# Scale and bias of the gating values: two GpSimd instructions become eight on VectorE

## What is computed

```python
def spatial_gating(z, ln_g, ln_b, w_s, b_s):
    u = z[..., :GMLP_WIDTH]
    v = layer_norm(z[..., GMLP_WIDTH:], ln_g, ln_b)      # 256 channels
    vs = v.reshape(bsz, n_s, GMLP_BLOCK, GMLP_HEADS, GMLP_HEAD_DIM)
    w = jnp.where(mask[None], w_s, 0.0)
    sv = jnp.einsum('hij,bsjhc->bsihc', w, vs) + b_s.T[None, None, :, :, None]
    return u * sv.reshape(bsz, t, GMLP_WIDTH)

def mixing_sublayer(x, ...):
    h = x @ w_in + b_in
    ...                                                  # c: conv group, att: attention
    gm = spatial_gating(jax.nn.gelu(h[..., OFF_GMLP:]), gmlp_ln_g, gmlp_ln_b, gmlp_w_s, gmlp_b_s)
    return jnp.concatenate([c, att, gm], axis=-1) @ w_out + b_out
```

## Time and profile before

| what | value |
|---|---|
| median of three runs | 943.93 us (942.88 to 945.69) |
| the profiled execution's own time | 938.3 us |
| its span in the profile | 936.5 us |
| mean granted clock of TensorE | 0.973 |
| TensorE busy with matmuls | 867.4 us (93%) |
| VectorE busy | 403.8 us (43%) |
| GpSimd busy | 300.3 us (32%) |

### The profile page before, as it was taken

One profiled execution on the slowest core, in us unless ns is written; L12 is line 12 of the kernel. 1 busy time (PEld: TensorE's weight loads), 2 busy tenths in 40 slices (PEclk: granted clock), 3 DMA queues, 4 the chain that ended last, 5 costly groups with the idle time before them and its releaser, 6 DMA issues.

```text
span 936.5 us, 15865 instructions
## 1 busy us (share of the span) xinstructions
PE 867.4 (93%) x5987; PEld 570.8 (61%) x5987; DVE 403.8 (43%) x924; ACT 253.6 (27%) x473; POOL 300.3 (32%) x223
## 2 busy tenths in 40 slices
PE   6999799889999998999999997998899999979995
PEld 5877578755555554555488776787555555545551
DVE  5997746732111111111559977467321111111126
ACT  5324842301111111111233248423012111111111
POOL 0632446222222221221534324462222222212233
PEclk9999899979999999999999998999799999999998
DMA  9761067799999999996814210677999999999955
GB/s 322 279 226 56 11 266 308 283 416 405 404 407 401 408 406 406 403 396 196 178 38 135 91 55 9 265 311 293 416 399 346 400 406 405 408 408 399 401 146 163
DMA packets 66278, 273.33 MB, mean 292 GB/s; under 512 B 8722, under 2 KB 24242, under 8 KB 41136
## 3 DMA queue, kind: packets, MB, share of 16 engines
q1 hardware_dynamic: 53792, 247.14, 66.1%
q0 software_dynamic: 12432, 25.41, 11.2%
HBM read 256.83 MB, written 22.02 MB: 298 GB/s over the span
## 4 chain that ended last, share of the span: by engine, by line
PE 65%; DVE 20%; DMA 10%; issue 2%; ACT 2%; POOL 0%; DVEq 0%; SPq 0%; ACTq 0%; POOLq 0%
PE bank L790 28%; PE bank L445 15%; PE bank L796 14%; DMA w_down<-in_exp_w_down 8%; DVE bank L1168 8%; PE bank L773 2%; DVE xTl L1137 2%; DMA moemem<-x_rows,first_tok 2%; DVE w_gate L1144 1%; PE bank L780 1%; PE bank L840 1%; PE bank L783 1%; DVE w_gate L1145 1%; DVE w_down L1143 1%; DVE xtok L1299 1%
## 5 line engine op out<-in xcount | busy, mean ns | idle before, releaser
L1414 DVE TENSOR_TENSOR moemem<-bank,moemem 64x128 f32<-64x128 f32 x172 | 48.3, 281 | 309.1 <-ACT moemem L1046 306.4
L1634 POOL DMA_INDIRECT moemem<-x_rows,gather_idx x43 | 44.9, 1045 | 284.5 <-DVE moemem L1428 260.4
L790 PE MATMUL bank<-w_up,moemem 128*64 128x256 f32 x1088 | 126.5, 386 | 2.2 <-DMA w_up<-in_exp_w_wide 2.2
L1581 POOL TENSOR_TENSOR wl<-w_gate,wh 128x2048 fp32r<-128x2048 f32 x17 | 78.0, 4590 | 126.4 <-ACT wh L909 98.4
L445 PE MATMUL bank<-xTh,wh 128*128 128x512 f32 (+1 forms) x256 | 101.1, 395 | 11.2 <-DVE xTl L1137 9.9
L790 PEld LDWEIGHTS bank<-w_up,moemem 128*64 128x64 f32 x1088 | 79.6, 140 | 47.1 <-issue 10.6
L1046 ACT ACTIVATE moemem<-bank 64x256 f32<-64x256 f32 x86 | 32.7, 381 | 246.3 <-PE bank L790 246.3
L445 PE MATMUL bank<-xTl,wh 128*128 128x512 f32 (+1 forms) x256 | 95.4, 373 | 0.0
L445 PE MATMUL bank<-xTh,wl 128*128 128x512 f32 (+1 forms) x256 | 95.2, 372 | 0.0
L1628 POOL DMA_INDIRECT y_rows<-moemem,scatter_idx x44 | 71.0, 1614 | 62.3 <-ACT moemem L1051 54.5
L790 PE MATMUL bank<-w_gate,moemem 128*64 128x256 f32 x736 | 83.4, 379 | 3.7 <-DMA w_gate<-in_exp_w_wide 3.7
(11 more groups left out here) (227 smaller groups left out, 1278.9 us busy)
## 6 DMA issues: line engine op xcount, KB each, us to landing
w_up<-in_exp_w_wide SPq DMA_DIRECT2D x24, 2048.0 KB
w_gate<-in_exp_w_wide SPq DMA_DIRECT2D x16, 2048.0 KB, 20.6
w_down<-in_exp_w_down SPq DMA_DIRECT2D x16, 2048.0 KB, 25.1
w_down<-in_exp_w_wide SPq DMA_DIRECT2D x8, 2048.0 KB
w_gate<-in_exp_w_down SPq DMA_DIRECT2D x8, 2048.0 KB
xtok<-in_exp_w_wide SPq DMA_DIRECT2D x8, 2048.0 KB, 24.4
moex<-in_exp_w_wide SPq DMA_DIRECT2D x8, 2048.0 KB
moew<-in_exp_w_down SPq DMA_DIRECT2D x8, 2048.0 KB
```

The lines of the kernel that those rows point to most:

```text
L790: return [pe.matmul(bank[i][CH * n:CH * n + CH, 0:256], x, w[:, 512 * n + 256 * i:512 * n + 256 * i + 256], start=(k == 0), stop=(k == KD ...
L1414: dve.tensor_tensor(he[CH * b:CH * b + CH, P * i:P * i + P], bank[i][0:CH, P * b:P * b + P], silu[:, 256 * i + P * b:256 * i + P * b + P], ...
L1581: pool.tensor_tensor(wl[(n + l) % SLOTS][:, :], wraw[n % 2], wh[(n + l) % SLOTS][:, :].bitcast(F32), ALU.subtract)\
L1634: return pool.indirect_dma_start(to, None, x1_halves[l], bass.IndirectOffsetOnAxis(ap=rows[:, :], axis=0), bounds_check=2 * T - 1, oob_is_ ...
```

## The change

GpSimd's two instructions go. VectorE's first four instructions no longer multiply by rstd but by `ln_g` (the first half of `rowm`), so they wait for `row_in` in place of `grstd_set`. Four further instructions multiply by rstd and add `ln_b`, in place in `gv`, behind `softmax_norm(l, 1)` and ahead of `heads_low(l, 0)`; each waits for the one before it (`link`). `gvn_set` is counted up behind them.

```diff
@@ VectorE
-                dve.wait_ge(grstd_set, l + 1)
-                for j in range(TT):
-                    link(dve.tensor_scalar(gv[:, j, :], gsrc[j], mv[:, 2 * j:2 * j + 1], rstd[:, j:j + 1],
-                                           ALU.subtract, ALU.mult))
+                dve.wait_ge(row_in, 16 * (l + 1))
+                for j in range(TT):
+                    link(dve.scalar_tensor_tensor(gv[:, j, :], gsrc[j], mv[:, 2 * j:2 * j + 1], rowm[:, 0:GM],
+                                                  ALU.subtract, ALU.mult))
                 dve.sem_inc(gvh_set, 1)
...
                 softmax_max(l, 2)
                 softmax_norm(l, 1)
+                dve.wait_ge(grstd_set, l + 1)
+                for j in range(TT):
+                    link(dve.scalar_tensor_tensor(gv[:, j, :], gv[:, j, :], rstd[:, j:j + 1], rowm[:, GM:2 * GM],
+                                                  ALU.mult, ALU.add))
+                dve.sem_inc(gvn_set, 1)
                 heads_low(l, 0)
                 copy_turned(l, 1)
                 conv_lows(l)
@@ GpSimd
-                pool.wait_ge(gvh_set, l + 1)
-                pool.wait_ge(row_in, 16 * (l + 1))
-                for i, op in ((0, ALU.mult), (1, ALU.add)):
-                    link(pool.tensor_tensor(gv, gv, rowm[:, GM * i:GM * i + GM].unsqueeze(1).broadcast_to([P, TT, GM]), op))
-                pool.sem_inc(gvn_set, 1)
                 pool.wait_ge(pn_done, TT * l + 2)
                 piece_lows(l, 8)
                 piece_lows(l, 9)
```

## The result

| kernel | median of 7, us | range | ratio to before (95% interval) |
|---|---|---|---|
| before | 943.93 | 940.8 to 945.69 | |
| changed | 951.18 | 949.33 to 955.43 | 1.0074 (1.0052 to 1.0096) |

The ratio makes 7.0 us. The changed kernel was timed twice more in other series, at 1.0082 (1.0054 to 1.0111) and 1.0077 (1.0046 to 1.0107). In one of these series a single execution of before took 1138.27 us at a mean granted clock of 0.744; it is left out everywhere. Forecast were 3.5 us, 947.4. The median of 951.18 lies 0.2 us above the range given (943.6 to 951.0); the ratio on the median of before gives 950.9, just inside.

What follows compares the result with a forecast made beforehand. TensorE was taken as the general bound, with VectorE counting where TensorE waits for the third block's probabilities. Two losses of 3.05 us less 2.60 gained made +3.5 on 943.93: 947.4 us, range 943.6 to 951.0.

Steps and rivals of the forecast that it cites:

- rival 3: TensorE idles longer, so one or two stretches at clock 0.50 reach later matmuls: +5.2 to +6.8, say 949.5 us; chance 0.14.
- The hold on the second four: GpSimd's piece 8 gets in behind the first, holding the second about 4.7 us; 10.38 us against 7.33, 3.05 lost a layer.
- the gap of 0.035 us: Between linked instructions of VectorE's second four: a waiting GpSimd gets in at the next gap, even one this short.
- The first four: VectorE's first four instructions in their new form: 0.48 us each, covered by TensorE's matmuls up to 102.96.
- `spatial` and `attend` cost nothing of their own: TensorE's two steps wait for the second four and the copy, but both come before the third block's probabilities.
- The gain of 2.60 us: VectorE's L1189 no longer held by GpSimd's two instructions: 2.11 us in the first layer, 0.49 in the second.
- the 2.11 us: First layer: L1189 would end at 105.81 in place of 107.92, no longer held by GpSimd's two instructions.
- The clock: TensorE's granted clock behind the third block's turn: no term in the +3.5 us sum, falls left to rival 3.
- Rival 1: VectorE keeps GpSimd out of all four; 1.72 us lost a layer, 2.60 gained: +0.8 us, 944.8; chance 0.18.
- Rival 2: Piece 8 no longer holds the `conv_lows` pair, which takes 1.28 us: -3.0 to -4.5 us, 940; chance 0.10.

Runs made afterwards that it cites:

- Piece 8 free: Changed kernel without GpSimd's wait for the second block's probabilities ahead of its piece 8; 941.52 us, ratio 0.9973 to before.
- piece 8 behind the four: Changed kernel with GpSimd's piece 8 waiting for the end of the second four instructions instead of the second block's probabilities; 949.04 us, ratio 1.0044 to before.
- the four without a wait between them: Changed kernel with only the last of the second four instructions waited for; 951.12 us, ratio 1.0065 to before.
- the matmuls for nothing: Changed kernel with 20 unneeded short matmuls on TensorE ahead of the second block's turn and 20 behind the fourth block's scores; 947.75 us, ratio 1.0025.
- the version with 20 matmuls: Changed kernel without GpSimd's wait ahead of piece 8, plus 20 unneeded matmuls ahead of the second block's turn; 939.57 us, ratio 0.992 to before.

## Why the prediction was right, and why the loss was twice its size

The direction came out by the mechanism forecast. The size is that of rival 3, the same hold with falls of the clock behind it ("+5.2 to +6.8"), which had a chance of 0.14, and not that of the forecast's own +3.5; that the time still falls at the edge of the range owes something to luck.

*The hold on the second four* was right in place, in who gets in first, and in size: one instruction of 4.63 us, and 10.30 us from block to block against the forecast 10.38. Piece 8 free and piece 8 behind the four show it by moving it. The reason given for GpSimd getting in was wrong: not the gap of 0.035 us behind a linked instruction, but, in every place seen here, that the side kept out has the next turn, as the four without a wait between them show.

*The first four* were 0.48 us each as taken, and covered. *`spatial` and `attend` cost nothing of their own*: right at full clock.

*The gain of 2.60 us* held for one execution and is somewhat too large in general. For the pair of executions that were compared it came out: the third block's turn is 0.87 us later in the first layer and 2.46 us in the second, +3.3 against the forecast +3.5. But the 2.11 us was the hold of one execution, in which TensorE had its full clock ahead of L575. In the second profile of before L1189 wasn't held in the first layer. There the change has nothing to give back. Over the profiles of each, the third block's turn is 3.7 us later (both layers). In the fourteen profiles of all versions L575 ended before 6.5 us in nine first layers and between 7.75 and 9.11 in the other five; by the 4.93 us above that is an average gain of 2.0 us for both layers, an estimate, in place of 2.60.

*The clock* is the term that was mis-sized: the sum has it at nothing, and rival 3 kept it apart. A stretch at the lower level reaches behind the third block's turn in all three profiles and costs 0.6 to 2.1 us over both layers, mean 1.6; the matmuls for nothing take it away. 3.7 + 1.6 = 5.3 us, of 7.0 to 7.7 timed. By the time of the kernel with these matmuls, whose executions had a mean granted clock of 0.975 where the changed kernel's had 0.963, the clock's share is larger, some 5 us, and what is left, 2.4 us, is no more than the forecast.

*Rival 1* (VectorE keeps GpSimd out of all four) did not occur, in no profile. The sentence of the Trainium skill beside it (SBUF — State Buffer, "A bandwidth-pool intuition that's wrong"), that a blocked claim resumes some 115 ns behind VectorE's end, is given there for the descriptors of a DMA and doesn't fit this case: piece 8 took 4.69 us against 4.52, begun at 112.32 while the first of the four ended at 112.64. It ran as if begun at 112.49, 0.15 us before that end. *Rival 2* did not occur in the changed kernel; it is what piece 8 free makes of it.

*Open:* some 2 us of the loss have no place in a profile. The profiled executions of the changed kernel were 1.1, 3.2 and 3.6 us faster than the medians of their series. The granted clocks of all executions point to TensorE's clock again. At the same mean granted clock (0.964 to 0.967) the changed kernel's executions took 3.3 to 4.4 us more than those of before, about the forecast sum. But it was lower more often: 7 of its 23 executions had 0.958 or less and took 953.7 us or more, where none of 86 of before had less than 0.961. None of these seven was profiled, so in which stages their clock fell isn't shown. In the expert stages the profiles differ by up to 2 us in both directions, with no sign for one kernel. Open too is why the version with 20 matmuls timed 5 us under what its profile explains.

## What to carry to other kernels

Before moving work off an idle engine, ask what else of that engine now stands beside the moved work: two inputs in SBUF on VectorE and a GpSimd instruction of 4.5 us cost 4.1 us of waiting in each layer, whoever has less to do. Place GpSimd's long instructions where VectorE works from PSUM or waits, which here was only a matter of dropping one wait. And a hold read from one execution may be a floor that takes up another engine's delays: take a second profile, measured from a point that the change can't move, before counting it as a gain. Where a change lets TensorE stand idle longer, put the clock into the sum and not beside it.

## What was not expected of the hardware

- Whoever had been kept out of the port had the next turn, even against instructions that follow each other without a gap: 4.74 us for the second of four unlinked ones.
- A scalar_tensor_tensor of 128x256 takes 0.485 us with both tensors in SBUF and about the same from PSUM (four linked in 2.04 us), against 0.544 for the tensor_scalar with two scalars from memory that it replaced.
- The granted clock ahead of L575 was 1.00 in some executions and 0.72 to 0.80 in others of the same kernel, which moved L575 by 1.6 to 2.4 us.
